# A two-layer transformer step on one core: twelve modulation GEMVs of the second layer done inside the first MLP, and the second layer's job orders written anew

## What is computed

```python
sh1, sc1, g1, sh2, sc2, g2 = ada_mods(cvec, p['w_ada'][li], p['b_ada'][li])   # silu(c) @ w_ada + b
h = rms_norm(x, p['norm_w'][li, 0]) * (1 + sc1) + sh1
x = x + g1 * y                                   # y: attention of h
h = rms_norm(x, p['norm_w'][li, 1]) * (1 + sc2) + sh2
x = x + g2 * sq_relu_mlp(h, p['w_mlp1'][li], p['w_mlp2'][li])
```

## Time and profile before

| | us |
|---|---|
| median of 3 runs | 1072.24 (1072.23, 1077.11, 1072.24) |
| profiled execution | 1076.48, span 1074.7 |
| granted clock, mean over the span | 0.982 of full |
| first MLP, PE from unit 19 to unit 48 | 311.42 to 564.03 |
| odd layer, norm to the start of u14 | 564.03 to 776.96 |
| rest of output projection and second MLP | 776.96 to the end |

### The profile page before, as it was taken

The page is one execution under the profiler, slowest core; times in us unless marked ns, Lnnn a source line. Parts: engine busy times, 40 slices in busy tenths (PEclk is TensorE's granted clock), DMA queues, the critical chain, the costliest instruction groups (busy, mean ns, idle before and its releaser), DMA issues.

```text
span 1074.7 us, 18015 instructions
## 1 busy us (share of the span) xinstructions
PE 1032.9 (96%) x7330; PEld 949.7 (88%) x7330; DVE 567.8 (53%) x907; ACT 488.9 (45%) x859; POOL 138.1 (13%) x168
## 2 busy tenths in 40 slices
PE   5899999999999999999999999989899999999997
PEld 2688886778999999999997988858799999999997
DVE  3464677564745354453557456556465535445352
ACT  4245565555544242342435446556545333243331
POOL 0052120002011010110100443240001011010110
PEclk9899999999999999999999999979999999999999
DMA  8778646644634334243343744040553434424311
GB/s 304 261 251 276 199 157 235 221 169 149 234 104 131 119 118 156 92 143 118 118 151 124 241 147 133 6 162 20 177 167 104 141 118 131 144 89 145 118 40 59
DMA packets 157099, 160.40 MB, mean 149 GB/s; under 512 B 3626, under 2 KB 155716, under 8 KB 157028
## 3 DMA queue, kind: packets, MB, share of 16 engines
q1 hardware_dynamic: 155028, 156.50, 44.1%
q0 software_dynamic: 528, 1.70, 0.4%
q10 hardware_dynamic: 1472, 1.18, 0.3%
HBM read 156.09 MB, written 3.28 MB: 148 GB/s over the span
## 4 chain that ended last, share of the span: by engine, by line
PE 89%; DVE 4%; ACT 3%; issue 2%; POOL 1%; DMA 0%; SPq 0%; DVEq 0%; ACTq 0%
PE G L546 61%; PE G L551 13%; PE TB L520 3%; PE OB L569 3%; PE SC L886 2%; PE OB L899 1%; PE TB L569 1%; ACT wH L991 1%; PE SC L662 1%; PE SC L589 1%; DVE wL L1448 1%; PE OB L683 1%; PE OB L753 1%; PE SC L638 1%; PE SC L632 1%
## 5 line engine op out<-in xcount | busy, mean ns | idle before, releaser
L991 ACT ACTIVATE wH<-raw 128x2048 fp32r<-128x2048 f32 x97 | 185.2, 1910 | 189.9 <-PE G L546 178.4
L546 PE MATMUL G<-opH,wH 128*128 128x386 f32 (+1 forms) x768 | 267.7, 349 | 3.0 <-DVE opL L1741 2.1
L546 PE MATMUL G<-opH,wL 128*128 128x386 f32 (+1 forms) x768 | 260.8, 340 | 0.0
L546 PE MATMUL G<-opL,wH 128*128 128x386 f32 (+1 forms) x768 | 260.4, 339 | 0.0
L1448 DVE TENSOR_TENSOR wL<-raw,wH 128x2048 fp32r<-128x2048 f32 x97 | 223.3, 2302 | 52.2 <-ACT wH L991 52.1
L546 PE MATMUL G<-hidH,wH 128*128 128x384 f32 x512 | 172.5, 337 | 0.0
L546 PE MATMUL G<-hidH,wL 128*128 128x384 f32 x512 | 172.1, 336 | 0.0
L546 PE MATMUL G<-hidL,wH 128*128 128x384 f32 x512 | 172.1, 336 | 0.0
L546 PEld LDWEIGHTS G<-opH,wH 128*128 128x128 f32 x768 | 145.1, 189 | 11.8 <-issue 5.6
L546 PEld LDWEIGHTS G<-opL,wH 128*128 128x128 f32 x768 | 144.9, 189 | 1.6
L546 PEld LDWEIGHTS G<-opH,wL 128*128 128x128 f32 x768 | 145.1, 189 | 0.0
(11 more groups left out here) (242 smaller groups left out, 1188.1 us busy)
## 6 DMA issues: line engine op xcount, KB each, us to landing
raw<-in_w_mlp SPq DMA_DIRECT2D x64, 1024.0 KB, 5.2
raw<-in_w_ada SPq DMA_DIRECT2D x48, 1024.0 KB, 5.5
raw<-in_w_in_even SPq DMA_DIRECT2D x13, 1024.0 KB, 5.6
raw<-in_w_in_odd SPq DMA_DIRECT2D x12, 1024.0 KB, 5.0
raw<-in_w_out_even SPq DMA_DIRECT2D x4, 1024.0 KB, 6.8
raw<-in_w_out_odd SPq DMA_DIRECT2D x4, 1024.0 KB, 6.5
xin<-in_x_sample SPq DMA_DIRECT2D x1, 1024.0 KB, 6.2
out_y_sample<-yout SPq DMA_DIRECT2D x1, 768.0 KB, 4.0
```

The lines of the kernel that those rows point to most:

```text
L546: mm = pe.matmul(G[:, s, 512 * m:512 * m + cols], w[:, s, k, P * m:P * m + P], a[:, k, 0:cols], start=first and q == 0, stop=last and q == 2)
L991: act.activation(wH[:, u % 2, :, :], raw[:, pos % RAW, :, :], ACT.Copy).then_inc(w_high, 1)
```

## The change

The twelve adaLN units 36 to 47 move in the stream, one behind each second unit of the first MLP from 20 to 42, and their PE steps into units 19, 21, ... 41: `ada_mm` after tile 2, `ada_turn` after tile 5. All go by OB. `ada_copy` and `ada` follow the splits of the unit before on ACT and DVE. The first MLP's loops become straight code on PE, ACT, DVE and SP, and a split that stood at the start of a group stands at the end of the one before. The three odd lists lose the adaLN entries and are written in a new order; the work that they name is otherwise the same.

```diff
-STREAM += [("u", _u) for _u in range(15, U_ODD + 2)]
-ODD_ADAS = {2: [36, 37], 3: [38], 4: [39], 5: [40], 6: [41], 7: [42], 8: [43], 9: [44], 10: [45], 11: [46], 12: [47]}
-GAP_ADAS = (36, 37)
+MLP_ADAS = {19: 36, 21: 37, 23: 38, 25: 39, 27: 40, 29: 41, 31: 42, 33: 43, 35: 44, 37: 45, 39: 46, 41: 47}
+for _u in range(15, U_ODD + 2):
+    STREAM += [("u", _u)] + ([("a", MLP_ADAS[_u - 1])] if _u - 1 in MLP_ADAS else [])
+ODD_ADAS = {}
...
 ODD_PE = """
-    ns5 kc0 ada36 ns6 adt36 ada37 kc1 adt37 u0.01 ada38 u0.22 adt38 u0.36 ada39 u0.77 adt39 u1.07 u2.07 ada40 u3.02
-    tt0 u3.33 tt1 u3.44 tt2 u3.55 tt3 d0 u3.67 d1 u4.00 dP0 u4.14 d2 u4.56 adt40 u4.77 u5.00 ada41 d3 PV0 u5.13 tt6
-    u5.47 tt7 d4 u6.00 adt41 u6.11 ada42 u6.23 tt8 u6.44 adt42 u6.55 ada43 d5 tt9 u6.66 dP1 u6.77 PV1 dP2 u7.03 d6 PV2
-    u7.44 dP3 u7.55 dN0 PV3 d7 u7.66 dP4 u7.77 u8.00 PV4 dP5 d8 u8.12 PV5 dP6 u8.33 d9 u8.44 dN1 u8.56 PV6 dP7 u8.77
-    tt14 PV7 d10 u9.01 dP8 u9.22 d11 tt15 PV8 u9.33 dP9 u9.45 PV9 dP10 u9.66 PV10 dP11 u9.77 PV11 u10.01 dN2 u10.23
-    dN3 u10.45 tt12 u10.66 d12 tt13 u10.77 adt43 d13 ada44 adt44 ada45 d14 tt18 tt19 d15 dP12 PV12 dP13 d16 PV13 dP14
-    tt20 PV14 d17 dP15 u11.00 PV15 dP16 u11.12 d18 PV16 tt21 u11.34 dP17 d19 u11.55 PV17 dP18 u11.67 d20 dN4 u12.00
-    dN5 u12.11 d21 PV18 u12.22 dP19 d22 u12.33 PV19 dP20 u12.44 d23 PV20 adt45 u12.55 ada46 dN6 dP21 PV21 dP22 u12.66
-    PV22 dP23 PV23 adt46 u13.00 dN7 u13.12 ada47 u13.33 u12.77 adt47 u13.47
+    ns5 kc0 ns6 kc1 u0.07 u1.07 u2.05 tt0 u2.66 tt1 u2.77 u3.06 tt2 u3.77 u4.00 d0 u4.11 tt3 u4.27 dP0 d1 u5.03 d2 tt6
+    PV0 u5.44 tt7 u5.56 d3 dP1 u5.77 PV1 dP2 d4 u6.00 PV2 tt8 u6.12 dP3 d5 tt9 PV3 u6.33 dN0 u6.44 d6 u6.56 d7 dP4
+    u6.77 u7.01 d8 PV4 dP5 u7.23 PV5 dP6 d9 u7.44 dN1 u7.55 PV6 dP7 u7.66 PV7 dP8 d10 u7.77 PV8 dP9 u8.00 d11 tt12
+    u8.12 tt13 u8.35 PV9 dP10 u8.66 PV10 dP11 u8.77 PV11 u9.00 dN2 u9.13 tt14 u9.44 tt15 d12 u9.55 dN3 u9.66 d13 dP12
+    u9.77 PV12 u10.00 d14 u10.11 dP13 u10.24 d15 PV13 u10.56 dP14 u10.77 PV14 dP15 d16 u11.00 tt18 u11.11 PV15 tt19
+    u11.22 d17 dN4 u11.34 dP16 u11.55 PV16 tt20 u11.66 dP17 d18 u11.77 tt21 PV17 d19 dP18 u12.00 PV18 d20 dP19 u12.11
+    dN5 PV19 d21 u13.01 d22 dP20 PV20 dP21 u12.22 d23 dN6 PV21 u12.34 dP22 u12.55 PV22 dP23 u12.66 PV23 u13.23 dN7
+    u13.46 u12.77 u13.77
...
 ODD_ACT = """
...
+    sp1 sq lam kc0 nr kc1 sh0 sh1 sh2 sh3 sh4 sh5 sh6 sh7 ev0 sp2 rs0 ev1 sp3 rs1 tt0 tt1 ev2 sp4 tt2 sp5 ev3 ex0 tt3
+    rs3 ev4 sp6 ex1 rs4 dP0 tt6 ex2 tt7 dP1 ex3 ev5 dP2 sp7 ex4 tt8 hr0 dP3 tt9 ex5 hn0 ex6 dP4 ex7 ev6 sp8 rs6 dP5
+    ex8 hr1 dP6 hn1 ex9 dP7 dP8 ex10 dP9 ev7 tt12 sp9 rs7 ex11 hr2 tt13 dP10 dP11 ev8 hr3 sp10 hn2 tt14 tt15 ex12 hn3
+    dP12 ex13 ev9 sp11 rs9 ex14 dP13 ex15 dP14 ev10 dP15 hr4 rs10 tt18 ex16 tt19 sp12 hn4 ex17 dP16 tt20 dP17 ex18
+    ev11 hr5 vo tt21 hh0 ex19 dP18 hh1 sp13 dP19 ex20 hn5 hh2 ex21 hh3 hh4 hh5 dP20 ex22 hr6 dP21 hn6 ex23 hh6 dP22
+    dP23 hr7 hn7 hh7
...
 ODD_DVE = """
...
+    scl lam sp1 lamb sc0 sc1 lo0 sc2 lo1 sc3 lo2 sc4 lo3 sc5 lo4 sc6 lo5 sc7 lo6 lo7 qn0 sp2 qs0 qn1 sp3 qs1 sp4 mx0
+    sp5 dw0 qn3 qs3 mx1 qn4 sp6 dw1 mx2 qs4 dw2 mx3 dw3 mx4 sp7 dw4 mx5 dw5 mx6 hs0 mx7 dw6 qn6 mx8 dw7 qs6 sp8 mx9
+    dw8 hs1 dw9 mx10 dw10 mx11 qn7 sp9 qs7 dw11 sp10 hs2 mx12 dw12 hs3 mx13 dw13 mx14 qn9 sp11 qs9 dw14 mx15 dw15 qn10
+    mx16 qs10 dw16 mx17 sp12 dw17 hs4 mx18 dw18 mx19 hl0 dw19 hl1 mx20 sp13 mx21 hs5 dw20 dw21 mx22 hl2 hl3 hl4 dw22
+    hl5 mx23 hs6 dw23 hl6 hs7 hl7
...
+                        if base + i in MLP_ADAS:
+                            a = MLP_ADAS[base + i]
+                            middle = {1: lambda: ada_turn(a)} if half else {2: lambda: ada_mm(a)}
...
-            with pe.Fori(0, 2) as g:
-                mlp_group(U_MLP0 + 8, g, 2 * KT, 4, MLP0_ORDER)
-            mlp_group(U_MLP0 + 24, 0, 2 * KT, 12, MLP0_ORDER)
+            for q in range(1, 4):
+                mlp_group(U_MLP0 + 8 * q, 0, 2 * KT, 4 * q, MLP0_ORDER)
...
-                    if i <= 5 or (i == 6 and not last):
-                        split_high(u + 2, pos + i + 2, g)
+                    if i < ends:
+                        split_high(u + 2, POS["u", u + 2], g)
+                    if u + 1 in MLP_ADAS:
+                        ada_copy(MLP_ADAS[u + 1])
...
+                    if u + 1 in MLP_ADAS:
+                        ada(MLP_ADAS[u + 1])
```

More of the change, by code:

```diff
@@ L192, in psum_uses @@
     sc.append("norm1")
+    for a in MLP_ADAS.values():
+        ob.append(f"ada{a}")
+        tb.append(f"ada{a}")
     for name in ODD_PE:
@@ L483, in _ @@
                     sp.dma_start(S0[:, :, :, :], t["state_hgrn"][0, 0].rearrange("d h k v -> k d h v")).then_inc(even_in, 16)
[L485 to L488, removed]
+            for pos in range(POS["u", U_MLP0], POS["u", U_ODD]):
+                kind, n = STREAM[pos]
+                if kind == "a":
+                    load_ada(n)
+                else:
+                    load(mlp_unit(0, (n - U_MLP0) % 8, (n - U_MLP0) // 8), pos)
             for pos in range(POS["u", U_ODD], POS["u", U_MLP1]):
@@ L849, in mlp_group @@
                         else:
-                            gemm_half(base + i, half, "fm", (hidH, hidL), ready, g=g)
+                            gemm_half(base + i, half, "fm", (hidH, hidL), ready, g=g, middle=middle)
                         if finish is not None and i > 4:
@@ L997, in ada_copy @@
             def ada_copy(a):
[L998 to L1003, removed]
+                full("ob", f"ada{a}")
+                act.activation(adarow[:, :], OB[:, 0:UC], ACT.Copy).then_inc(ob_free, 1)
             def square(n, k):
@@ L1282, in _, with mlp_group @@
             norm_rstd(1)
-            def mlp_group(base, g, pos, n_hid, last, turned_out=None, finish=None):
+            def mlp_group(base, g, n_hid, late, ends, turned_out=None, finish=None):
                 for i in range(8):
                     u = base + i
-                    if i == 0 and n_hid % 16:
-                        split_high(u + 1, pos + 1, g)
+                    if i == 0 and late:
+                        split_high(u + 1, POS["u", u + 1], g)
                     if turned_out is not None and i > 4:
@@ L1313, in _ @@
             act.wait_ge(out_dma, 16 * 3)
[L1314 to L1318, removed]
+            for q in range(3):
+                mlp_group(U_MLP0 + 8 * q, 0, 4 * q, False, 8)
+            mlp_group(U_MLP0 + 24, 0, 12, False, 7,
                       finish=lambda u, tile0: squares(2, u, tile0) if tile0 < 6 else None)
@@ L1772, in _, with mlp_group @@
             dve.wait_ge(out_dma, 16 * 3)
-            def mlp_group(layer, base, g, pos, n_hid, last, summed=None):
+            def mlp_group(layer, base, g, n_hid, late, ends, summed=None):
                 for i in range(8):
                     u = base + i
-                    if i == 0 and n_hid % 16:
-                        split_low(u + 1, g, pos + 1)
+                    if i == 0 and late:
+                        split_low(u + 1, g)
                     if i < 4:
@@ L1794, in mlp_group @@
                         residual(u, G2, layer, 2 * (i - 4), g)
-                    if i <= 5 or (i == 6 and not last):
-                        split_low(u + 2, g, pos + i + 2)
+                    if i < ends:
+                        split_low(u + 2, g)
+                    if u + 1 in MLP_ADAS:
+                        ada(MLP_ADAS[u + 1])
                     if summed is not None and i >= 4:
                         square_sums(summed, (2 * i - 8, 2 * i - 7))
-            b0, b1 = POS["u", U_MLP0], POS["u", U_MLP1]
             dve.wait_ge(mods_set, 24)
-            mlp_group(0, U_MLP0, 0, b0, 0, False)
-            with dve.Fori(0, 2) as g:
-                mlp_group(0, U_MLP0 + 8, g, b0 + 8, 4, False)
-            mlp_group(0, U_MLP0 + 24, 0, b0 + 24, 12, False, 2)
+            for q in range(3):
+                mlp_group(0, U_MLP0 + 8 * q, 0, 4 * q, False, 8)
+            mlp_group(0, U_MLP0 + 24, 0, 12, False, 7, 2)
             def lambda_sums():
```

43 lines of the change are left out of this document (14 added, 29 removed).

## The result

| | before | after |
|---|---|---|
| median (lowest to highest), 10 runs each | 1073.12 (1071.93 to 1077.11) | 1068.72 (1064.68 to 1070.58) |
| ratio, 95% interval | | 0.9949 [0.9933, 0.9965] |
| profiled execution (span) | 1076.48 (1074.7) | 1066.31 (1064.5) |
| granted clock, mean | 0.982 | 0.992 |

The two medians differ by 4.4 us; the ratio on record, 0.9949, is not their quotient (0.9959) and makes 5.5 us, with an interval of 3.8 to 7.2. The kernel is faster beyond the interval. The interval lies on both sides of the half per cent that the prediction took as its bound, and 1068.72 lies inside its band of 1066.9 to 1077.6.

What follows compares the result with a forecast made beforehand. PE's work plus PE's losses were taken to bound the kernel. 14.9 - 3.3 - 9.2 - 17.7 + 3.1 + 1.0 = -11.2 us, from a median of 1072.24 to 1061.0, range 1053 to 1070.

Steps and rivals of the forecast that it cites:

- the half per cent: What a measurement can tell from no change: 5.4 us, giving a no-change band of 1066.9 to 1077.6.
- 1. First MLP: First MLP: twelve adaLN units come in at 1.24 each, +14.9 us, bounds 14 and 16, no waits.
- B: First MLP, units 19 to 42: loads bound it and the kernel gets slower, 1085 us; chance 0.04.
- D: First MLP: the turn waits for the copy, 1 us in each of six units, +6, 1067 us; chance 0.04.
- 2. Norm and u0: Odd layer's norm and u0: first tile earlier, DVE gives a tile each 1.44 us; -3.3 us, bounds +1.5 and -3.6.
- the two tiles named as a sign: Behind the odd layer's norm: the prediction is wrong if the clock stays low for more than two tiles.
- 3. u1 to u14: Odd layer, u1 to u14: -9.2 us of PE work, and losses before u14 of 7.0 instead of 24.7, -17.7.
- 4., the hand-over: Before u14: its split waits for u12's last tile, a wait of 3.5 instead of 0.4; +3.1 us, bounds 2.5 and 4.
- Rival A: Odd layer's attention: splits on ACT and DVE delay blocks, 9 us come back, 1070 us; chance 0.14.
- the 165 named as a sign: Odd layer: the prediction is wrong if u13 ends later than 165 us after u1's start.
- 5. The clock: Behind the wait before u14: some 3 us at the lower clock would cost 1.5; taken as +1.0 us, between 0 and 2.

## Why the prediction was right or wrong

**The bound.** Right: PE's work and PE's losses set the time, before and after.

**1. First MLP: wrong, +17.0 instead of +14.9,** outside the bounds of 14 and 16, and so one of the prediction's own signs of being wrong. The step that failed is the price of an adaLN unit, 1.24, in which the `ada_mm` has one break of 0.10 and the `ada_turn` none. In the changed kernel, inside unit 19:

```profile
310.68 0.34 PE L549 MATMUL G<-opH,wL 128*128 128x386 f32 x1
310.95 1.07 PE L571 MATMUL OB<-raw,cst 128*32 128x256 f32 x16
311.95 0.45 PE L549 MATMUL G<-opH,wH 128*128 128x386 f32 x1
312.24 0.34 PE L549 MATMUL G<-opL,wH 128*128 128x386 f32 x1
...
315.24 0.38 PE L523 MATMUL TB<-ident,adarow 128*128 128x128 f32 x2
315.38 0.42 PE L549 MATMUL G<-opH,wH 128*128 128x386 f32 x1
315.63 0.33 PE L549 MATMUL G<-opL,wH 128*128 128x386 f32 x1
```

GEMM matmuls follow one another at 0.18. From the last one to the `ada_mm` it is 0.27 (+0.09), the `ada_mm` is 1.00, and the first matmul behind it keeps PE 0.29 (+0.11). The turn is 0.14, and the matmul behind it 0.25 (+0.07). The sum is 1.41; twelve are 16.9. The hint stood in the earlier trace rows: the matmul behind each job has 0.38 and 0.37 where the one before has 0.28, and the reading start to start stopped at its start. In that trace the matmul behind it follows 0.22 and 0.20 later, instead of 0.12:

```profile
577.17 0.38 PE L551 MATMUL G<-wH,opH 128*128 128x256 f32 x1
577.39 0.28 PE L551 MATMUL G<-wH,opL 128*128 128x256 f32 x1
...
578.48 0.37 PE L551 MATMUL G<-wH,opH 128*128 128x256 f32 x1
578.68 0.28 PE L551 MATMUL G<-wH,opL 128*128 128x256 f32 x1
```

That the trial with two units fewer gave 2.8 confirms the price. PE is busy for all 269.60 us of the MLP, so no wait on the copy appeared and none on the loads: rivals B and D were false.

**2. Norm and u0: right, -2.85 against -3.3.** The first tile came 7.99 after the norm's sum, 8.40 before: 0.4 earlier where I had taken about 0.5. The wait in front of it is now 3.36, and DVE's 1.44 a tile covers the low clock, which held for less than the two tiles named as a sign.

**3. u1 to u14, with 4., the hand-over: the sum is right, in part by luck.** The terms give 191.3 - 9.2 - 17.7 + 3.1 = 167.5 (the 168.5 under "What would show it" fits only with the clock's 1.0 added), and it took 168.03. PE is idle 5.7 us of it. Of these 3.35 are the wait before u14, forecast as 3.5. The other waits are 2.4, where the prediction had 3.0 + 1.5. PE's busy time is 162.3, where the work and the pitch had 157.0 + 2.5. So the waits came out 2.1 lower and the work 2.8 higher, and the two misses nearly cancel; what the 2.8 are no run shows. The mechanism is right: the two losses of the old order are gone, and what remains is small (PE's waits from 577 to 765: what for, us in total, times, longest):

```profile
PE G L554 <- DVE opL L1493: 3.4, 1, 3.4
PE G L549 <- DVE wL L1447: 3.4, 1, 3.4
...
PE G L549 <- DVE opL L1740: 0.8, 1, 0.8
PE OB L902 <- ACT DPT L1334: 0.6, 1, 0.6
```

The first stands at the norm and the second before u14; no wait in the attention is over 0.8. From 700 to 725 PE is busy all 25.00 us at full clock. Rival A was false: u13 ends 164.7 after u1's start, just inside the 165 named as a sign. The trial of the move alone shows that this came from the order: without it a wait of 3.48 stands at a block's scores.

**5. The clock: wrong, +2.8 instead of +1.0.** The step is "some 3 us at the lower level would cost 1.5: I take +1.0, between 0 and 2". The wait left 6 us at 1.2 GHz, not 3, and the cost is outside my bounds. The rows gave three cases: the stretch at the norm, at a clock of 0.92, holds 21.63 x 0.08 / 0.5 = 3.5 us at the lower level, the one from 754.57 at 0.84 holds 10.47 x 0.16 / 0.5 = 3.4, and the one from 702.18 at 0.71 holds 23.47 x 0.29 / 0.5 = 13.6. I went by the smaller ones alone, took 1.0 of their 1.5 without a reason, and the upper bound should have reached to the third. In none of the three was PE empty for as long as 3 us at a time (the longest wait is 1.92). The Trainium skill ("TensorE: Matmul & The Clock Gate", "What's actually happening") has the throttled state as the default that activity releases. The trace agrees: with PE kept occupied the stage takes 23.34, with 3.35 us of nothing 26.12; my 2.0 for "that rule alone" was still 0.8 short.

**The sum.** The two steps that failed are the price of a unit (2.1) and the clock (1.8); sections 2 and 3 add 0.45 and 0.5. Together they are 4.9, which takes -11.2 to -6.3. The ratio says 5.5 and its interval of 3.8 to 7.2 holds the 6.3. Of the 7.7 between 1061.0 and 1068.72, 4.9 are these terms, 0.9 is the before of the comparison, at 1073.12 instead of 1072.24, and 1.9 stay open. They are smaller than what single executions vary by, as unit 19 begins anywhere from 307.4 to 313.2 and the old odd stretch took 188.5 to 191.6.

**The chances.** The kernel is faster, but by the bound of half a per cent the runs do not decide between "faster", at 0.80, and "same", at 0.14. A case was missing, in which two prices in a kernel where PE has no room are each a little too small; with 12 units, 0.17 each is 2 us.

## What to carry to other kernels

Where PE is the bound, price a job that is put into a run of matmuls up to the second matmul behind it, and multiply the break by the count before deciding where it goes: the same unit cost 1.41 in the run and about 0.2 in a wait. Ask of each wait on PE what the clock does behind it: the two before u14, of 3.35 and 2.30 us, cost 2.8 and 1.5 more through the clock, where PE sets the pace; the one of 3.36 at the norm cost nothing more, where DVE does; and the waits of at most 0.8 in u1 to u14 left the clock at 1.00. Work that must be done anyhow belongs in the long ones, and a few idle matmuls, no longer than the wait, are the next best. Compare two profiles stage by stage from a point that both share, since untouched code can differ by nearly as much as the change.

## What the runs showed of the hardware that was not expected

- A wait of 3.35 us on PE was followed by 6 us at 1.2 GHz (2.8 us lost); a wait of 2.30 by a stretch that lost 1.5 (24.89 against 23.34). Five matmuls whose result nobody reads, 3.39 us in all, brought the loss to 0, with a DMA share of 1.05 beside them.
- A run of GEMM matmuls that is broken by another job loses 0.09 ahead of and 0.11 behind a 1.00 us `ada_mm`, and 0.07 behind two transposes.
- The same program's executions differ by 5.7 us in where unit 19 starts (307.53 and 313.24 in two executions of the kernel after), and the granted clock in sparse stretches differs with it, 0.97 and 0.89 in 12 to 72, as does what the DMA moves there, 285 and 255 GB/s. Why it differs stays open.
- Straight code in place of the hardware loop changed nothing on PE: the eight units with four adas take 73.04, which is 67.40 and four times 1.41.
